# Inverting the 64-token blocks of a delta rule: the masked factors are made on GpSimd instead of VectorE, and TensorE waits on two semaphores instead of one

## The reference, cut to what matters

```python
def rwkv7_scan(r, w, k, v, kk, ak, s0):
    def step(s, inp):
        r_t, w_t, k_t, v_t, kk_t, ak_t = inp
        sa = jnp.einsum('bhvk,bhk->bhv', s, kk_t)
        s = s * w_t[:, :, None, :] - sa[..., None] * ak_t[:, :, None, :] + v_t[..., None] * k_t[:, :, None, :]
        return s, jnp.einsum('bhvk,bhk->bhv', s, r_t)
```

## Time and profile before

| | us |
|---|---|
| median of 3 runs | 1832.45 |
| lowest and highest run | 1829.4, 1833.08 |
| span of the profiled execution | 1830.5 |
| groups 0 and 1, levels 1 to 5 and their work beside | about 1190 to 1245 |
| groups 2 and 3, `products` to level 5 | about 1255 to 1308 |

### The profile page before, as it was taken

How to read it: one execution, slowest core, us unless ns; L and a number is a source line. 1 busy time by engine, 2 the same in 40 slices (tenths; PEclk the granted TensorE clock), 3 DMA queues, 4 the chain that set the end, 5 groups by cost and what they waited for, 6 DMA issues and landing times.

```text
span 1830.5 us, 33169 instructions
## 1 busy us (share of the span) xinstructions
PE 1612.4 (88%) x14721; PEld 1307.1 (71%) x14721; DVE 884.3 (48%) x1211; ACT 633.6 (35%) x818; POOL 135.6 (7%) x105
## 2 busy tenths in 40 slices
PE   8999999999999999999989999989998656556566
PEld 6999998998799999899879896778854222212221
DVE  4445566665444456566655867996633111101111
ACT  4345444544434454454454222434413000000100
POOL 0600000000060000000003460000000000000000
PEclk9999999999999999999999999999999878877888
DMA  8553366755576426677533340100099999999998
GB/s 299 194 185 116 139 228 247 258 188 196 193 273 236 150 106 220 248 269 242 192 106 93 93 112 12 25 3 3 4 398 380 425 426 427 425 425 425 428 425 339
DMA packets 130263, 418.70 MB, mean 229 GB/s; under 512 B 14170, under 2 KB 35485, under 8 KB 111186
## 3 DMA queue, kind: packets, MB, share of 16 engines
q1 hardware_dynamic: 129698, 416.50, 60.0%
q10 hardware_dynamic: 432, 0.22, 0.0%
HBM read 414.81 MB, written 1.89 MB: 228 GB/s over the span
## 4 chain that ended last, share of the span: by engine, by line
PE 63%; DMA 17%; DVE 9%; ACT 5%; SPq 5%; issue 2%; DVEq 0%; ACTq 0%
PE bank L1346 33%; DMA R<-w_exp_gate 12%; SPq L1239 4%; PE bank L1933 3%; PE bank L1515 3%; PE ps_s L1461 3%; PE ps_t L1461 3%; DMA R<-w_exp_down 2%; PE bank L1533 2%; PE ps_t L1515 2%; PE ps_s L1515 2%; ACT w_high L1998 2%; PE ps_s L1533 1%; DVE w_low L2475 1%; PE ps_t L1533 1%
## 5 line engine op out<-in xcount | busy, mean ns | idle before, releaser
L2475 DVE TENSOR_TENSOR w_low<-wring,w_high 128x2048 fp32r<-128x2048 f32 (+1 forms) x127 | 288.2, 2269 | 302.3 <-ACT w_high L1998 301.9
L1998 ACT ACTIVATE w_high<-wring 128x2048 fp32r<-128x2048 f32 (+1 forms) x127 | 236.3, 1860 | 331.9 <-PE bank L1346 299.4
L1346 PE MATMUL bank<-x_high,w_high 128*128 128x256 f32 x1600 | 322.4, 283 | 7.9 <-DVEq L2526 7.9
L1346 PE MATMUL bank<-x_low,w_high 128*128 128x256 f32 x1600 | 320.2, 282 | 0.0
L1346 PE MATMUL bank<-x_high,w_low 128*128 128x256 f32 x1600 | 318.3, 280 | 0.0
L1346 PEld LDWEIGHTS bank<-x_high,w_high 128*128 128x128 f32 x1600 | 244.6, 190 | 13.9 <-DVEq L2526 8.8
L1346 PEld LDWEIGHTS bank<-x_high,w_low 128*128 128x128 f32 x1600 | 246.4, 189 | 0.0
L1346 PEld LDWEIGHTS bank<-x_low,w_high 128*128 128x128 f32 x1600 | 245.4, 189 | 0.0
L1933 PE MATMUL bank<-R 128*32 128x512 f32 x640 | 140.0, 704 | 112.7 <-DMA wring<-w_exp_up 71.8
L1933 PEld LDWEIGHTS bank<-R 128*32 128x32 f32 x640 | 35.1, 127 | 205.4 <-issue 127.3
L1933 PE MATMUL bank<-wring,R 128*32 128x512 f32 x384 | 139.7, 701 | 0.0
(11 more groups left out here) (691 smaller groups left out, 2863.3 us busy)
## 6 DMA issues: line engine op xcount, KB each, us to landing
wring<-w_in SPq DMA_DIRECT2D x29, 2048.0 KB, 8.2
R<-w_exp_up SPq DMA_DIRECT2D x24, 2048.0 KB, 37.5
R<-w_exp_down SPq DMA_DIRECT2D x24, 2048.0 KB, 44.2
wring<-w_up SPq DMA_DIRECT2D x22, 2048.0 KB, 8.2
R<-w_exp_gate SPq DMA_DIRECT2D x16, 2048.0 KB, 35.1
wring<-w_exp_gate SPq DMA_DIRECT2D x16, 2048.0 KB, 33.3
wring<-w_ada SPq DMA_DIRECT2D x12, 2048.0 KB, 10.4
wring<-w_down SPq DMA_DIRECT2D x10, 2048.0 KB, 7.9
```

What stands on the lines that cost most here:

```text
L1346: mm = pe.matmul(b[:, i * S:(i + 1) * S], left, right, start=k == 0 and m == 0 and i == 0, stop=k == last and m == 2, skip_group_check=True)
L1998: a.activation(high_of(l, job), half_block(l, job, wring), ACT.Copy).then_inc(w_high_ready, 1)
L2475: v.tensor_tensor(half_block(l, job, w_low), half_block(l, job, wring), high_of(l, job).bitcast(F32), ALU.subtract).then_inc(w_low_ready, 1)
```

## The change

GpSimd, idle since L3314, makes the `MT` of levels 2 to 5 for each group: 16 products of 128 x 512. It waits for T1 of the level before and raises `next_masked`. VectorE loses those 16 products (L2906), the 16 memsets (L2916) and the waits for its own update of `XT` (at all levels, the fifth too). TensorE waits before T1 of level n > 1 for `next_masked` and for the update of `X` of level n - 1, and before the updates of level n > 1 for that of `XT` of level n - 1, as well as for T1's copy as before. For level 1 it waits for `inverse_begun`, raised by L2891. In `products` the first mask (L2885) is now followed by a wait for its completion before L2886 is issued, where the wait stood one instruction later.

```diff
 def inverse_inputs(g, n):
-    return 10 * (g // 2) + 2 * (n - 1) + g % 2 + 1
+    return 8 * (g // 2) + 2 * (n - 2) + g % 2 + 1
...
@@ TensorE, group_step
                     n = int(stage[-1])
-                    pe.wait_ge(mt_ready, inverse_inputs(g, n))
+                    if n == 1:
+                        pe.wait_ge(inverse_begun, g + 1)
+                    else:
+                        pe.wait_ge(next_masked, inverse_inputs(g, n))
+                        wait_emptied2(pe, ("XU", 8 * g + n - 1))
                     b = fill("T1", 8 * g + n)
                     heads64(b, every, cc_(w.MT), cc_(w.X)).then_inc(full2, 1)
                 else:
                     n = int(stage[-1])
                     wait_emptied2(pe, ("T1", 8 * g + n))
+                    if n > 1:
+                        wait_emptied2(pe, ("XTU", 8 * g + n - 1))
...
@@ VectorE, group_step, products
-                    v.tensor_tensor(w.MT[:, :, :], w.LT[:, :, :], mask(2, dr), ALU.mult).then_inc(m0_done, 1)
+                    chain(v.tensor_tensor(w.MT[:, :, :], w.LT[:, :, :], mask(2, dr), ALU.mult))
                     chain(v.tensor_tensor(w.X[:, :, :], b3(("L1", g)), mask(8, dr), ALU.mult))
-                    v.wait_ge(m0_done, g + 1)
...
-                    v.tensor_tensor(w.MT[:, :, :], w.LT[:, :, :], mask(3, dr), ALU.mult).then_inc(mt_ready, 1)
+                    v.tensor_tensor(w.MT[:, :, :], w.LT[:, :, :], mask(3, dr), ALU.mult).then_inc(inverse_begun, 1)
...
-                elif stage[0] == "M" and stage != "MX5":
-                    n = int(stage[-1])
-                    wait_full2(v, ("T1", 8 * g + n))
-                    v.tensor_tensor(w.MT[:, :, :], w.LT[:, :, :], mask(3 + n, dr), ALU.mult)
                 elif stage[0] == "X":
...
                     v.tensor_tensor(w.XT[:, :, :], w.XT[:, :, :], b3(("XTU", 8 * g + n)), ALU.subtract)\
                         .then_inc(dve_emptied2, 1)
-                    wait_emptied2(v, ("XTU", 8 * g + n))
-                    if n < 5:
-                        v.memset(st[:, 63:64], 0.0).then_inc(mt_ready, 1)
...
@@ GpSimd, at its end
+            def mask_next(g, n):
+                dr, w = g // 2, work[g % 2]
+                m = 9 * dr + 3 + n
+                wait_full2(g_eng, ("T1", 8 * g + n))
+                g_eng.tensor_tensor(w.MT[:, :, :], w.LT[:, :, :], rw_mask[:, m:m + 1, :].broadcast_to([P, NCH, 64]), ALU.mult)\
+                    .then_inc(next_masked, 1)
+
+            for step, g in MIXER_STEPS:
+                if step == "group" and g[0][0] == "M" and g[0] != "MX5":
+                    mask_next(g[1], int(g[0][-1]))
```

## The result

| | before | changed |
|---|---|---|
| median | 1831.88 us (4 runs, 1829.40 to 1833.08) | 1838.91 us (4 runs, 1837.64 to 1842.56) |
| span of the profiled execution | 1830.5 | 1836.3 (its time is 1838.13) |
| ratio, with its 95% interval | | 1.0038 (1.0022 to 1.0055) |

A forecast was written before the change was run, and what follows sets the result against it. VectorE and TensorE in turns were taken to bound groups 0 and 1, TensorE nearly alone groups 2 and 3. Terms 0.2 + 0 + 0.55 + 0 + 1.65 - 0.2 - 0.4 = +1.8 on 1832.45 gave 1834.3 us, range 1829.0 to 1837.2.

The forecast's parts named there:

- Who collides, and for how long: VectorE products with two SBUF operands wait for GpSimd's masks, taken as 1.2 us each; reads from banks pay nothing.
- Products: In `products`, L2886 now waits for L2885: 0.11 us per group, on the path for each pair's second group, +0.2.
- Level 1: Two masks leave VectorE, saving 1.22 us; waits for GpSimd at rope cost 1.1 to 1.2; net 0.
- Level 2, the collision: L2844 waits for GpSimd's mask and ends 0.85 us later, delaying logits, copy and TensorE; net for the level +0.55.
- Level 3: Group 1's mask leaves VectorE, saving 0.6 us, but L2857 waits 0.6 for GpSimd's mask; net 0.
- Level 4, the collisions: L2860 waits 0.75 us and L2862 1.15 for GpSimd's masks; less 0.25 from shorter waits, net +1.65.
- The collisions together: In groups 0 and 1, pieces and rope together wait 3.9 us for GpSimd's masks.
- the clock stays up in the likeliest case: TensorE's clock does not fall behind the longer pause at level 4; forecast +1.8 us in all, chance 0.42.
- partly hidden: Argument against a clock loss: where VectorE sets the time, a slower TensorE costs less than its full +1.7 us.
- Groups 2 and 3, -0.4: No pieces, hardly a collision, masks off the path; TensorE's waits for the memset go, gaining 0.4 us.
- The clock falls as well: Rival: level 4's pause of 3.2 to 3.5 us halves TensorE's clock, +1.7 us, to 1836.0; chance 0.22.
- No collisions: Rival: GpSimd's masks miss VectorE's products, -2.5 us, or -4.1 to 1828.4 if the clock stays up; chance 0.15.

The follow-up runs named there:

- a3: Changed kernel plus five useless matmuls filling TensorE's pauses, two at level 2 and three at level 4: 1835.69 us, ratio 1.0020.
- part 1: Not a run: the stretch of groups 0 and 1, first `near` matmul to that of `near` 24; 62.52 us before, 68.26 changed.
- part 2: Not a run: the stretch of groups 2 and 3, `near` 24 to the first 128x36 matmul behind the mixer; 67.25 us before, 66.32 changed.
- before again: The kernel before, unchanged, profiled a second time: 1828.77 us (1 run).
- changed again: The changed kernel, unchanged, timed and profiled a second time: 1839.05 us, ratio 1.0038.
- d2: Changed kernel plus three useless matmuls in TensorE's pause at level 4 alone: 1835.65 us, ratio 1.0016.
- d3: Changed kernel with one `prepare` piece moved from ahead of level 4's reciprocal to behind level 4's T1: 1832.45 us, ratio 1.0003.
- a4: Changed kernel with GpSimd's masks waiting for the update of `X` instead of for T1: 1830.31 us, ratio 0.9994.
- c4: Changed kernel with GpSimd's 16 products replaced by memsets to zero, which alters the result: 1830.98 us, ratio 0.9994.

## Why the prediction was wrong, point by point

- **Who collides, and for how long: right.** VectorE's pieces and rope wait until GpSimd's product ends (1.44 to 1.65 us instead of 0.69), the updates and logits from banks keep their 0.68 and 0.41. The mask takes 1.28, taken as 1.2. The memset run shows that it is the read.
- **Products: right.** The second product starts 0.73 us behind the first instead of 0.61: 0.12, worked out as 0.11.
- **Level 1: right,** -0.14 us (1197.20 - 1188.82 against 1198.28 - 1189.76), worked out as 0, one collision against two masks.
- **Level 2, the collision: right in size.** From the first `near` to group 1's updates +0.82, for +0.85.
- **Level 3: right.** From T1 of level 3 (1211.45 before, 1212.41 after) to VectorE's next update of `X` (1218.83, 1219.88) +0.09, worked out as 0. L2857 (now L2864) waits as worked out, 1.06. T1 of level 4 itself starts 0.6 to 0.7 sooner behind that update, since TensorE no longer waits for `XT`'s; the prediction said so, and that it is worth nothing.
- **Level 4, the collisions: right within 0.2.** From the update of `X` ahead of it (1218.83, the row of before below this point) to the transposes it was 5.21 us, from its counterpart (L2912 at 1219.88) it is 6.66: +1.45, for +1.65. The gain of 0.25 ahead of the pieces is there (L2910 to L2860 2.64 us, L2912 to L2867 2.39), and the two waits were 0.75 and 0.94, for 0.75 and 1.15. Counted from T1 it looks like +2.13, because T1 now starts sooner.

```profile
1218.83 0.68 DVE L2910 TENSOR_TENSOR wring<-wring,ps_s 128x512 f32<-128x512 f32 x1
```

- **The collisions together: right.** With the clock held at levels 2 and 4 (a3) part 1 is 1.95 us longer than before: +0.53 to T1 of level 3 (worked out 0.55), +0.10 to the update of `X` (0), +1.46 to the transposes (1.65), -0.14 behind them (-0.2). This is a net figure. The five VectorE products waited 4.2 us in all (the prediction's 3.9 leaves out L2857's 0.6, which its terms have), and against the memset run, with 1.4 off for the clock at level 1, they cost 8.38 + 64.47 - 1.4 - (7.44 + 59.75) = 4.3.
- **The step that failed: that the clock stays up in the likeliest case, and that if it falls it falls at level 4 alone, for +1.7.** Level 4 was seen, by the comparison with the earlier trace rows, but given a chance of 0.22, though its pause was worked out as 3.2 to 3.5 us and the only row of such a pause showed a fall; "partly hidden" should not have counted so much. It cost 2.3 us, since the clock was down for about 6.6 us and not 3.4 (13.2 in all, less 3.3 each for levels 1 and 2), of which the first 1.3 still lay in the pause. Level 2 was not seen at all: the prediction worked out that its pause grows from 1.22 to about 2.1 us and asked nothing about the clock behind it. It cost 1.5. Both together, 3.8 us, are twice the 1.95 that were left of the collisions.
- **Groups 2 and 3, -0.4: not there.** Part 2 is 64.8 to 64.9 us in every profile in which the clock didn't fall, with VectorE's masks (64.79, 64.79) or GpSimd's (64.90, 64.90, 64.91); what there is, is +0.1. TensorE never waits for GpSimd in the changed kernel.
- **The rivals.** "The clock falls as well" is what happened, short by a second place and by the length of the first: with 3.8 instead of 1.7 it would have given 1838.1, against 1838.9. "No collisions" has its measure in the memset run: -3.9 us from T1 of level 1 to `near` 24, with the pause down to 2.29 and the clock up, near the -4.1 forecast for that case; its median of 0.9994 (0.9984 to 1.0003) doesn't show it.

**What stays open.** Part 1 accounts for 5.8 of the 7.0 us between the medians (7.0 in the 7 later runs as well); the rest is within their intervals. The part behind the mixer differs by 1 to 2 us between profiles (502.5 before, 504.0 before again, 504.5 changed, 503.9 changed again, 505.2 with the clock held at levels 2 and 4, 501.9 to 504.3 in the others), which I can't give to a program. And what decides over the clock besides the length of a pause is open. Behind 2.24 to 2.25 us at level 2 it fell in all four profiles that have this pause (changed, changed again, d2, d3), behind 2.28 and 2.29 at level 1 (a4, c4) in neither, and ahead of `near` 25 behind 3.36 to 3.48 in nine of eleven.

## What to carry to other kernels

When a stall on one engine makes TensorE's pause longer, price the pause twice: once as time, and once for the granted clock behind it, at every place where the pause grows, and compare each with the pauses of the same trace behind which the clock did and didn't fall; here pauses of up to 1.3 us in the kernel before were free, and the clock behind pauses of 2.25 and 3.53 cost 3.8 us, twice what the stalls left as a net loss. Before a product is given to GpSimd, look for what VectorE does in that moment: a product of two SBUF operands waits until GpSimd's has ended, a read from a bank doesn't, and a wait on a later event or a piece moved behind what TensorE waits for takes the cost away. Then ask what the offloading is to bring: even masks that cost nothing shorten their stretch by 3.9 us, 0.2% of this kernel, which its median did not show.

## What the runs showed of the hardware that was not expected

- The granted clock fell to the 1.2 GHz level behind a pause of only 2.25 us at level 2, at the same place in all four profiles that have it (2.24 or 2.25), and stayed for some 3.3 us; at level 4, behind 3.53 us, for some 6.6 us.
- The same program with the same pause of 3.36 us ran the matmuls behind it once at half speed (1.98 us for 16) and once at full speed (1.09): part 2 was 67.25 or 64.79 us long, a third of the change's whole effect by chance.
- A few matmuls with no use in a pause held the clock: two at level 2 and three at level 4 gave back 3.8 us, and TensorE then still waited 0.3 to 0.8 us, so they were in nobody's way. Three ahead of the first `near` with the later masks were in the way by 0.4 us.
- GpSimd's memset of 128x512 took 0.52 us and cost a VectorE product beside it nothing; its product took 1.28 us, 1.9 times VectorE's 0.69, and two in a row with VectorE's between them 2.94 to 3.12.
